# The last network's inner products as seven block products per pair of hidden tiles

## The reference, cut to what matters

```
def swiglu(h, w_in, w_out):
    gate, up = jnp.split(h @ w_in, 2, axis=-1)
    return (jax.nn.silu(gate) * up) @ w_out
x = residual_post_norm(x, swiglu(modulate(x, m, 2), ffn2_w_in, ffn2_w_out), m[:, 8], FFN_HALF, ln_gain[2], ln_bias[2])
```

## Time and profile before

| | us |
|---|---|
| median of 3 runs (lowest to highest) | 1334.32 (1333.84 to 1335.79) |
| the profiled execution | 1336.66 |
| its span, first to last instruction | 1334.8 |

### The profile page before, as it was taken

One profiled execution on the slowest core, in us unless ns is written; L12 is line 12 of the kernel. 1 busy time (PEld: TensorE's weight loads), 2 busy tenths in 40 slices (PEclk: granted clock), 3 DMA queues, 4 the chain that ended last, 5 costly groups with the idle time before them and its releaser, 6 DMA issues.

```text
span 1334.8 us, 17708 instructions
## 1 busy us (share of the span) xinstructions
PE 1307.2 (98%) x7134; PEld 1102.9 (83%) x7134; DVE 825.3 (62%) x1165; ACT 546.5 (41%) x740; POOL 83.0 (6%) x91
## 2 busy tenths in 40 slices
PE   8999999999999999999999999999999999999996
PEld 5778888888889999888888888887788888888885
DVE  5446688666686777565227678878763223335888
ACT  5525221222212544565325645556552222224553
POOL 1000000000000000000202221220000000000000
PEclk8999999999999999999999999999999999999998
DMA  9965545665545667553432478266435333333562
GB/s 320 275 180 175 186 164 164 185 180 172 178 158 156 177 189 190 174 174 126 138 122 64 83 200 220 54 148 150 142 95 158 95 111 95 96 95 110 190 205 102
DMA packets 217378, 206.74 MB, mean 155 GB/s; under 512 B 7322, under 2 KB 175880, under 8 KB 216592
## 3 DMA queue, kind: packets, MB, share of 16 engines
q1 hardware_dynamic: 202328, 151.39, 38.5%
q0 software_dynamic: 14272, 52.53, 13.9%
q10 hardware_dynamic: 696, 1.68, 0.4%
HBM read 203.46 MB, written 25.18 MB: 171 GB/s over the span
## 4 chain that ended last, share of the span: by engine, by line
PE 84%; DVE 6%; ACT 3%; issue 2%; DMA 2%; SPq 2%; DVEq 0%; ACTq 0%
PE ps L2199 27%; PE ps L2201 26%; PE ps L2200 26%; DMA w_raw<-ffn_w_in 1%; DVE w_lo L1448 1%; DMA gain_bias_b<-w_ada 1%; PE ps L2238 1%; SPq L770 1%; PE ps L2662 1%; PE ps L2647 1%; ACT w_hi L957 1%; PE ps L2251 0%; PE ps L2681 0%; SPq L766 0%; DVE xl L1570 0%
## 5 line engine op out<-in xcount | busy, mean ns | idle before, releaser
L2199 PE MATMUL ps<-h_hi,w_lo 128*128 128x512 f32 (+1 forms) x1120 | 391.5, 350 | 1.9 <-DVE w_lo L1796 1.4
L2201 PE MATMUL ps<-h_hi,w_hi 128*128 128x512 f32 (+1 forms) x1120 | 387.7, 346 | 0.0
L2200 PE MATMUL ps<-h_lo,w_hi 128*128 128x512 f32 (+1 forms) x1120 | 387.7, 346 | 0.0
L1448 DVE TENSOR_TENSOR w_lo<-w_raw,w_hi 128x2048 fp32r<-128x2048 f32 (+1 forms) x116 | 256.3, 2210 | 157.9 <-ACT w_hi L957 157.7
L957 ACT ACTIVATE w_hi<-w_raw 128x2048 fp32r<-128x2048 f32 (+1 forms) x116 | 214.2, 1848 | 274.0 <-PE ps L2201 259.9
L2199 PEld LDWEIGHTS ps<-h_hi,w_lo 128*128 128x128 f32 x1120 | 211.7, 189 | 32.2 <-issue 4.2
L2201 PEld LDWEIGHTS ps<-h_hi,w_hi 128*128 128x128 f32 x1120 | 211.7, 189 | 27.0
L2200 PEld LDWEIGHTS ps<-h_lo,w_hi 128*128 128x128 f32 x1120 | 211.8, 189 | 25.5
L2199 PE MATMUL ps<-w_hi,h_lo 128*128 128x512 f32 x298 | 117.0, 393 | 1.4 <-DVE w_lo L1448 1.4
L1460 DVE SCALAR_TENSOR_TENSOR ada_row<-ada_block,c_cols,ada_row 128x256 f32<-128x256 f32 x224 | 108.6, 485 | 8.0
L2199 PE MATMUL ps<-h_hi,half_lo 128*128 128x512 f32 (+1 forms) x272 | 101.9, 375 | 0.7 <-ACT beside_lo L1286 0.4
(11 more groups left out here) (297 smaller groups left out, 1699.5 us busy)
## 6 DMA issues: line engine op xcount, KB each, us to landing
w_raw<-ffn_w_in SPq DMA_DIRECT2D x124, 512.0 KB, 5.2
ada_block<-w_ada POOLq DMA_DIRECT2D x28, 1024.0 KB, 5.7
w_raw<-ffn_w_out SPq DMA_DIRECT2D x55, 512.0 KB, 4.3
weight_sums<-ffn_w_out POOLq DMA_DIRECT2D x6, 2816.0 KB, 21.6
half_raw<-w_mix_in SPq DMA_DIRECT2D x48, 256.0 KB, 3.4
w_raw<-weight_sums SPq DMA_DIRECT2D x20, 512.0 KB, 4.0
ada_block<-w_ada SPq DMA_DIRECT2D x6, 1024.0 KB, 9.7
weight_sums<-weight_sums POOLq DMA_DIRECT2D x2, 2816.0 KB, 17.9
```

What stands on the lines that cost most here:

```text
L1448: nc.vector.tensor_tensor(lo, raw, hi.bitcast(F32), ALU.subtract).then_inc(s_lo[s], 1)
L2199: nc.tensor.matmul(dst, s_low, m_high, start=start, stop=False, skip_group_check=shared)
L2200: nc.tensor.matmul(dst, s_high, m_low, start=False, stop=False, skip_group_check=shared)
L2201: return nc.tensor.matmul(dst, s_high, m_high, start=False, stop=stop, skip_group_check=shared)
```

## The change

Tiles 0 to 3 (`WHOLE = 4`) stay inner jobs as before. Tiles 4 to 21 become nine pairs (`PAIRS = 9`) of two tiles: 512 tokens are cut in two halves, the 1024 channels of h in two halves, and gate and up (256 columns each) are the two column halves. The 2 x 2 by 2 x 2 block product is formed with seven block products; each is 2 x 4 k tiles x 3 = 24 matmuls of 256 moving columns. A pair has four jobs (parts): (P1, P5), (P6, P3), (P7, P2), (P4). Part 0 loads 1 MB (a block of w_in and a block of a sum in DRAM), part 1 0.5 MB, part 2 1 MB; part 3 loads nothing. The weights of P6 and P4 are formed by VectorE in `w_raw` (`add_inner_weights`). The sums in DRAM (`inner_weight_sums`) are made by GpSimd's queue: eight copies of 1.18 MB behind the blocks m = 11, 13, ... 25 in the first network, four additions of 1.18 MB behind m = 28, 30, 32, 34, and four in the mixer (groups 1, 2, 2, 4). Four block sums of h are formed on VectorE and split before and during tiles 0 to 3. In the outer product P2 and P7 change places, and P7 is copied out by ScalarE and joined from SBUF. The core of the diff:

```diff
-SEVEN = ("P1", "P5", "P6", "P3", "P7", "P2", "P4")
+SEVEN = ("P1", "P5", "P6", "P3", "P2", "P7", "P4")
+PAIR_PARTS = (("P1", "P5"), ("P6", "P3"), ("P7", "P2"), ("P4",))
+PAIR_BANKS = ({"X": 0, "Y": 1, "Z": 2}, {"X": 3, "Y": 6, "Z": 7})
+def raw_before(i):
+    return max((j for j in range(i) if j % 2 == i % 2 and (loads_raw(j) or JOBS[i][1:2] != ("pair",))), default=None)
 SyncE, load(i):
                 sp.wait_ge(s_lo[slot_of(before)], USES[before] + 1)
+                if key[1:2] == ("pair",):
+                    if part == 0:
+                        sp.wait_ge(s_wadd, 2 * t_)
+                        sp.wait_ge(s_isum, 64)
+                        sources = (w2i[:, 0:4, c0:c0 + 256], i_sums[0][...])
+                    elif part == 1:
+                        for k in (0, 2):
+                            sp.dma_start(blocks[:, 1, k:k + 2, :], w2i[...]).then_inc(s_loaded[s], 16)
+                        return
+                    else:
+                        sp.wait_ge(s_wadd, 2 * t_ + 1)
+                        sp.wait_ge(s_isum, 128)
+                        sources = (i_sums[1][...], w2i[:, 4:8, c0:c0 + 256])
+                    for b, src in enumerate(sources):
+                        sp.dma_start(blocks[:, b, :, :], src).then_inc(s_loaded[s], 16)
-                if key == ("L2", "in", 0, 6):
+                if key == ("L2", "pair", 1, 0):
                     gain_bias(2)
 GpSimd:
             for m in range(ADA_FIRST, ADA_BLOCKS):
                 ada(m)
+                if 11 <= m < 27 and m % 2:
+                    copy_inner(n // 4, n % 4)
+                if m >= 28 and m % 2 == 0:
+                    pool.wait_ge(s_icopy, 128)
+                    add_inner(0, (m - 28) // 2)
+                for n in {1: (0,), 2: (1, 2), 4: (3,)}.get(g, ()):
+                    add_inner(1, n)
 ScalarE, for each pair t and part:
+                        pair_split_hi(JOB["L2", "pair", t, part] + 2)
+                        if part == 0: pair_keep(t, "P1"); pair_keep(t, "P5")
+                        if part == 1: pair_keep(t, "P6")
+                        if part == 3: pair_silu(t, 0); pair_silu(t, 1)
 ScalarE, outer jobs:
-                    if n in (3, 6, 9):
+                    if n in (3, 6, 9, 18):
                         keep(SEVEN[n // 3 - 1], 1)
                     split_both_hi(n + 2)
-                    if n in (2, 5, 8):
+                    if n in (2, 5, 8, 17):
                         keep(p, 0)
 VectorE:
+            def pair_split_lo(i):
+                split_lo(i)
+                if JOBS[i][3] == 2:
+                    add_inner_weights(JOBS[i][2], 1)
+                for t in range(PAIRS):
+                    for part in range(len(PAIR_PARTS)):
+                        pair_split_lo(JOB["L2", "pair", t, part] + 2)
+                        if part == 1:
+                            pair_join(t, "P3")
+                        if part == 2:
+                            pair_join(t, "P7")
+                            if t + 1 < PAIRS:
+                                add_inner_weights(t + 1, 0)
+                            pair_join(t, "P2")
+                    pair_hidden(t, 0)
+                    pair_hidden(t, 1)
+                    first_left_sums(t)
 TensorE, pair_products(t, part): ready(i), then for each product
+                    if p in ("P6", "P3", "P7"):
+                        pe.wait_ge(s_kept, 3 * t + ("P6", "P3", "P7").index(p) + 1)
+                    if p == "P4":
+                        pe.wait_ge(s_joined, 3 * t + 2)
```

More of the change, by code:

```diff
@@ L65, in ffn @@
         for part, tiles in enumerate(FFN_PARTS[tag]):
-            jobs.extend((tag, "in", part, j) for j in range(tiles))
+            jobs.extend((tag, "in", part, j) for j in range(WHOLE if tag == "L2" else tiles))
             if tag == "L2":
+                jobs.extend((tag, "pair", t, part) for t in range(PAIRS) for part in range(len(PAIR_PARTS)))
                 jobs.extend((tag, "seven", p, s) for p in SEVEN for s in range(len(SEVEN_STEPS)))
@@ L164, in out_keys @@
     if tag == "L2":
-        return [(tag, 0, half, i) for half, tiles in ((1, (0, 1)), (1, (2, 3)), (0, (0, 1)), (0, (2, 3))) for i in tiles]
+        return [(tag, 0, half, i) for half, tiles in ((1, (0, 1)), (0, (0, 1)), (1, (2, 3)), (0, (2, 3))) for i in tiles]
     tiles = TC if tag == "C" else TL
@@ new lines, in pair_silu, with pair_split_hi @@
+            def pair_silu(t, late):
+                if late:
+                    wait_done(JOB["L2", "pair", t, 3])
+                    act.wait_ge(s_hf, pair_hid(t))
+                    nc.scalar.activation(glu[:, 1, :], ps[:, pair_bank(t, "P4"), :], ACT.Silu).then_inc(s_silu, 1)
+                else:
+                    act.wait_ge(s_joined, 3 * t + 3)
+                    nc.scalar.activation(glu[:, 0, :], glu[:, 0, :], ACT.Silu).then_inc(s_silu, 1)
+            def pair_split_hi(i):
+                if i >= SEVEN_FIRST:
+                    split_both_hi(i - SEVEN_FIRST)
+                else:
+                    split_hi(i)
@@ new lines, in input_sum_low, with add_inner_weights @@
+            def input_sum_low(n):
+                p, slot = (("P5", 0), ("P6", 1), ("P7", 1), ("P3", 0))[n]
+                dve.wait_ge(s_lefthi, n + 1)
+                hi, lo = pair_left(p)
+                nc.vector.scalar_tensor_tensor(out=lo, in0=h_sums[slot][:, :, :], scalar=left_sign(p), in1=hi.bitcast(F32),
+                                               op0=ALU.mult, op1=ALU.subtract).then_inc(s_leftlo, 1)
+            def add_inner_weights(t, which):
+                first, second, third = (JOB["L2", "pair", t, part] for part in range(3))
+                blocks = [w_raw[s][:, :].rearrange("p (b n) -> p b n", n=1024) for s in (first % 2, second % 2)]
+                if which == 0:
+                    if t:
+                        last = JOB["L2", "pair", t - 1, 3]
+                        dve.wait_ge(s_lo[slot_of(last)], USES[last] + 1)
+                    for i in (first, second):
+                        dve.wait_ge(s_loaded[i % 2], 32 * RAW_LOADS[i])
+                    a, b = blocks[0][:, 1, :], blocks[1][:, 1, :]
+                else:
+                    dve.wait_ge(s_loaded[third % 2], 32 * RAW_LOADS[third])
+                    dve.wait_ge(s_lo[slot_of(second)], USES[second] + 1)
+                    a, b = blocks[1][:, 0, :], blocks[0][:, 1, :]
+                nc.vector.tensor_tensor(blocks[1][:, 0, :], a, b, ALU.add).then_inc(s_wadd, 1)
```

266 lines of the change are left out of this document (205 added, 61 removed).

## The result

| us | before | after |
|---|---|---|
| median of 4 runs (lowest to highest) | 1334.34 (1333.84 to 1335.79) | 1352.43 (1351.6 to 1353.0) |
| the profiled execution | 1336.66 | 1351.6 |
| its span | 1334.8 | 1349.8 |

The ratio is 1.0133, with an interval of 1.0116 to 1.0151. The prediction (1335, range 1325 to 1343) missed on the slow side.

The account below looks back on a forecast made before the run. The loop of loads, not TensorE, was taken to set the pairs' pace. Pairs -0.8, `gate_b` load +0.7, end +0.35, GpSimd's queue +0.5 sum to +0.75 us on 1334.32, about 1335; range 1325 to 1343.

Parts of the forecast that it names:

- GpSimd's queue: First network and mixer: the copies and additions of the sums cost 0 to 4 us together, taken as 0.5.
- Rival 3: The pieces on GpSimd's queue hold up the first network or the mixer: +4 us, 1339; chance 0.1.
- The first network's cover: VectorE's own idle time ahead of the weights, 49.9 us, covers 6.5 us more of waiting for late modulation blocks.
- TensorE's part: Pairs: 168 matmuls at 0.120 us, 20.16 us a pair against 21.76; 14.4 us gained over nine if nothing else sets the pace.
- the loop: Pairs: loads, splits, sums and join in two buffers make rounds of 21.86 us, above TensorE's 20.16; 0.8 of 14.4 us stay.
- one stall at P4 a pair: Pairs: TensorE stalls about 1.7 us a pair ahead of P4, waiting for VectorE's join of P7.
- a `keep` is the bound: Sign of a wrong prediction: stalls at products other than P4 mean a `keep` or a split is the bound; no size given.
- `gate_b`: Pairs: the ACT queue's load of it behind pair 3 touches the loop once, 0.7 us added.
- gain and bias rows: Pair 1: SyncE's 1 MB between the loads of parts 0 and 1 has room; nothing added.
- The end and the order of P2 and P7: Outer product: ScalarE copies P7's second bank before splitting the last weights; +0.35 us, bounds -0.5 to +1.
- rival 1: Pairs: loads are as quick as TensorE needs, 4.35 us, so the loop stays out of the way; -12.9, 1321.5; chance 0.2.

Follow-up runs that it names:

- the pieces alone: The kernel before with all sixteen pieces (eight copies, eight additions) at the places of the change and nothing reading the sums; 1352.86 us, ratio 1.0129.

## Why the prediction was wrong, step by step

**The step that failed** is "GpSimd's queue": "four more add perhaps 5 us of waits, of which TensorE sees little. Together 0 to 4 us, I take 0.5." What TensorE saw was 14.7 us in the mixer of the changed kernel, 15.5 for the pieces alone, 13.4 and 12.8 by the medians when the mixer's four are taken out or moved (18.1 less 4.7 and 5.3). Rival 3 named the mechanism and gave it 4 us and a chance of 0.1; its price was nearly four times too low. Two readings were at fault. I added the additions' durations to waits that ScalarE already has, and took the small total of waits for slack. The row that mattered was not read: a load in the mixer that landed after up to 18.0 us, when TensorE just did not wait. And I had no term for what is queued ahead. The addition's own size, 7.3 us, was not the error: in the first network the four additions land 11.7 to 13.7 us after their issue where 12 follow from it, and in the mixer the backlog ends 197.2 us after the mixer's start with the addition and about 189 without. But behind two transfers of 2.8 MB it lands 37.1 us after its issue, and the loads beside it are slow until then. Nor had I a term for TensorE's clock, which falls to the lower level behind each of the two waits.

**The first network's cover** held in the trace of the changed kernel. Between 300 and 350 us TensorE was busy for 49.96 of 50 us at a DMA share of 0.82, and between 200 and 400 it stood still for 0.04 us (0.00 before). That it holds in general is not shown. Two other executions with the same pieces have 0.65 us of idle time there (without the mixer's additions) and 1.97 (the pieces alone), and in the latter VectorE waited 14.0 us for modulation blocks, where it waited 6.3 before and I had forecast 6.5 more. The mark of the mixer's start goes both ways, 637.32 before, and 635.76, 635.90, 636.52 and 639.54 with the pieces, and these are single executions. The twelve pieces cost between nothing and some 2 us, and no run has them alone.

**TensorE's part and the loop** were right in the main: pitch 0.12 us, one stall at P4 a pair, released by the join, in eight of nine pairs, and the rounds are those I had worked out. The stalls at P4 are 0.98 to 1.40 us and not 1.7. Four at P6, 3.1 us together, are what the prediction had put down as a sign that a `keep` is the bound; they stand where part 2 came late, and all twelve together make 13.0 us, against 8 x 1.7 = 13.6. From P4's start to P4's start:

| pair to pair | us |
|---|---|
| 1 to 2, 2 to 3 | 21.87, 21.85 |
| 3 to 4, with the `gate_b` load | 22.65 |
| 4 to 5, 5 to 6 | 21.93, 21.92 |
| 6 to 7, 7 to 8 | 22.60, 22.23 |
| 0 to 1, with the gain and bias rows | 22.9 (pair 0 has no stall: its P4 put at 1035.57 + 20.16 - 2.88) |

`gate_b` costs 0.8 us, forecast 0.7. The **gain and bias rows**, to which I gave "room", cost about 1.1: their megabyte lies between part 0's load and part 1's, and the sum waits 1.41 us for the latter:

```profile
1053.69 1.22 DVE L1882 TENSOR_TENSOR w_raw<-w_raw 128x1024 f32<-128x1024 f32 x1 [1.41 <-DMA w_raw<-ffn_w_in]
```

The 22.60 has a load that landed after 6.0 us instead of 5.4, with no other transfer that the profile shows; why stays open. Together these make 198.4 us from tile 3's silu to the last one, where I had 195.7; before took 196.4. That the loop is the bound is shown by what broke it: two edits that only change what a load waits for and when a sum is made took 15.1 us off (1340.44 to 1325.35).

**The end and the order of P2 and P7**: -0.15 us for a forecast of +0.35, and alone no difference that can be told from nothing.

**What the prediction had no term for**: rival 1 was discussed as loads that are quicker than I took them. They weren't (5.0 and 5.4 us against my 5.2). What was to be had lay in the order of waits.

## What to carry to other kernels

Read the longest landings of small loads, not only the waits: here a load took five times its usual time, nobody but ScalarE waited for it, and it had no room left. The next transfer behind a backlog in another queue was paid in full, and the clock that fell behind the wait came on top. Put DRAM-to-DRAM work where the DMA share is low and no long transfer stands ahead (0.23 here at 700 us), not where its inputs happen to be ready. Where a loop of load, split and sum sets the pace, walk it in program order. Here it came out within 0.1 us in the rounds that nothing else touched, and each thing that the next load need not wait for was worth its time once a round, until the next bound (here P4's join) was reached.

## What was not expected of the hardware

- 256 KB of weights in short rows took 24.2 us beside GpSimd's backlog (median of such loads 3.5 us), landing within 0.5 us of the backlog's end. The packets of the two queues were equal in number, 575 and 578, at 2 KB and 0.5 KB each.
- Behind the same backlog an addition in DRAM of 1152 KB landed in 37.1 us and a plain copy in 34.8.
- Behind waits of 5.7 and 6.3 us TensorE's granted clock was 0.50 and 0.52, and its pitch with 512 columns 0.427 us instead of 0.227, for 3 to 5 us of work.
- Cutting the additions' rows to 1 KB stopped GpSimd for 19 us ahead of the issue, with nothing that the profile shows to wait for.
- A megabyte in 1 KB rows is there 5.0 to 5.4 us after its first issue. With the first half issued 1.1 and 1.7 us ahead of the second, it is there 5.1 and 4.7 us after the second.
